# Two transformer blocks on one core: buffers at new places, cross attention in a new order, and small products moved

## The reference, cut to what matters

```python
x = x + 0.5 * swiglu(rmsnorm(x, ffn1_norm), ffn1_wgu, ffn1_wdown)
h = rmsnorm(x, mix_norm);  z = h @ w_in            # attention and convolution, gated, merged, @ w_out
x = x + merged @ w_out
x = x + 0.5 * swiglu(rmsnorm(x, ffn2_norm), ffn2_wgu, ffn2_wdown)
x = x + sigmoid(rmsnorm(x, ple_gate_norm) @ ple_gate_w) * rmsnorm(p @ ple_proj, ple_norm)
# second block
proj = rmsnorm(h, norm_mix_g) @ w_in_2             # q, k, v (short convolution), z, b, a, pool
h = h + concat(pool_mixer, gated_delta_rule) @ w_out_2
m = rmsnorm(mem, mem_norm_g)
q, k, v = rmsnorm(h, g) @ w_xq, m @ w_xk, m @ w_xv
h = h + (softmax(q k^T / 16) v) @ w_xo
h = h + relu(rmsnorm(h, g) @ w_up)**2 @ w_down
return rmsnorm(h, final_norm_g)
```

## Time and profile before

| | |
|---|---|
| median of 3 runs | 2119.24 us |
| the profiled execution: its time | 2118.75 us |
| its span | 2116.6 us |
| mean granted TensorE clock | 0.989 |
| HBM read and written | 241 MB, 33 MB |

### The profile page before, as it was taken

How to read it: one execution, slowest core, us unless ns; L and a number is a source line. 1 busy time by engine, 2 the same in 40 slices (tenths; PEclk the granted TensorE clock), 3 DMA queues, 4 the chain that set the end, 5 groups by cost and what they waited for, 6 DMA issues and landing times.

```text
span 2116.6 us, 25119 instructions
## 1 busy us (share of the span) xinstructions
PE 2056.2 (97%) x9682; PEld 1676.8 (79%) x9682; DVE 1230.4 (58%) x1737; ACT 831.3 (39%) x1268; POOL 5.9 (0%) x11
## 2 busy tenths in 40 slices
PE   7999999999899999999999999999998999999997
PEld 6888888887677787888888877789977778888886
DVE  5676575478998445554444565588563445544534
ACT  5444343334765443422222344334353433222211
POOL 0000000000000000000000000000000000000000
PEclk9999999999999999999999999999999999999998
DMA  7999884544234442333232321210143222322221
GB/s 255 297 296 304 271 291 162 184 162 154 100 114 146 159 149 93 127 100 100 90 99 93 99 88 60 70 41 16 34 136 100 96 74 98 101 90 99 90 100 60
DMA packets 80340, 275.09 MB, mean 130 GB/s; under 512 B 8928, under 2 KB 11360, under 8 KB 80224
## 3 DMA queue, kind: packets, MB, share of 16 engines
q1 hardware_dynamic: 79648, 272.72, 38.8%
q10 hardware_dynamic: 576, 0.79, 0.1%
HBM read 240.97 MB, written 32.51 MB: 129 GB/s over the span
## 4 chain that ended last, share of the span: by engine, by line
PE 87%; DVE 7%; ACT 3%; issue 2%; DMA 0%; DVEq 0%; ACTq 0%
PE ps L327 26%; PE ps L331 26%; PE ps L328 26%; DVE cacc L1697 2%; PE ps L349 1%; PE ps L647 1%; PE ps L640 1%; ACT whi L945 1%; PE ps L341 1%; PE ps L803 1%; PE ps L820 1%; DVE scr L2016 1%; DVE scr L1629 1%; DVE wlo L1587 0%; PE ps L480 0%
## 5 line engine op out<-in xcount | busy, mean ns | idle before, releaser
L327 PE MATMUL ps<-Hh,whi 128*128 128x512 f32 x1528 | 607.9, 398 | 23.6 <-DVE Hl L1615 11.1
L331 PE MATMUL ps<-Hh,wlo 128*128 128x512 f32 x1528 | 600.0, 393 | 2.5 <-DVE wlo L1587 2.5
L328 PE MATMUL ps<-Hl,whi 128*128 128x512 f32 x1528 | 599.3, 392 | 0.0
L945 ACT CAST whi<-raw 128x1024 fp32r<-128x1024 f32 (+3 forms) x352 | 350.4, 1001 | 361.4 <-PE ps L331 332.7
L1587 DVE TENSOR_TENSOR wlo<-raw,whi 128x1024 fp32r<-128x1024 f32 (+3 forms) x294 | 338.3, 1157 | 192.6 <-ACT whi L945 189.6
L327 PEld LDWEIGHTS ps<-Hh,whi 128*128 128x128 f32 x1528 | 289.6, 190 | 93.2 <-issue 15.9
L331 PEld LDWEIGHTS ps<-Hh,wlo 128*128 128x128 f32 x1528 | 289.4, 189 | 66.1 <-DVE wlo L1587 4.9
L328 PEld LDWEIGHTS ps<-Hl,whi 128*128 128x128 f32 x1528 | 289.4, 189 | 60.4 <-issue 1.7
L1697 DVE SCALAR_TENSOR_TENSOR cacc<-upad,gains,cacc 128x512 f32<-128x512 f32 x232 | 157.8, 744 | 0.0
L1653 DVE SCALAR_TENSOR_TENSOR x<-ps,x 128x512 f32<-128x512 f32 x80 | 55.3, 691 | 175.5 <-PE ps L331 175.4
L327 PE MATMUL ps<-f3Ah,whi 128*128 128x512 f32 x256 | 101.3, 396 | 0.0
(11 more groups left out here) (327 smaller groups left out, 2747.5 us busy)
## 6 DMA issues: line engine op xcount, KB each, us to landing
raw<-in_w SPq DMA_DIRECT2D x369, 512.0 KB, 4.0
low_parts<-lo SPq DMA_DIRECT2D x58, 512.0 KB, 4.7
wlo<-low_parts SPq DMA_DIRECT2D x58, 512.0 KB, 3.4
raw<-in_w SPq DMA_DIRECT2D x16, 384.0 KB, 3.0
raw<-in_w SPq DMA_DIRECT2D x17, 256.0 KB, 2.6
out<-x SPq DMA_DIRECT2D x8, 256.0 KB, 2.1
x<-in_x SPq DMA_DIRECT2D x5, 256.0 KB, 6.4
raw<-in_w SPq DMA_DIRECT2D x8, 128.0 KB, 2.0
```

The source lines that it names most:

```text
L327: e.matmul(out, h[:, kk, :], a, start=part != "last" and k + kk == 0, stop=False)
L328: e.matmul(out, h[:, kk, :], c, start=False, stop=False)
L331: ins = e.matmul(out, lo[:, kk, :], a, start=False, stop=done)
L945: e.copy(whi[i % WS][:, 0:n], raw[i % RAWS][:, 0:n]).then_inc(*act.tick("whi", ("whi", i)))
```

## The change

It moves the stage buffers, gives `P` a second buffer, pairs two products at the start of mix2, reorders cross attention on all engines and shifts some norms' parts. No instruction's kind or size is changed.

```diff
 # places: 16 KB "LOW" right behind Hl (where raw and whi began), x and raw behind the PB region
         RAWS, WS = 3, 3
-        x = glob("x", [128, 8, T])
         Hh, Hl = glob("Hh", [128, 8, T], F32R), glob("Hl", [128, 8, T], F32R)
-        raw = [glob(f"raw{i}", [128, 1024]) for i in range(RAWS)]
+        LOW = cursor[0]
+        cursor[0] += 16384
         whi = ...
         wlo = ...
+        PB = cursor[0]
+        cursor[0] += 83584
+        x = glob("x", [128, 8, T])
+        raw = [glob(f"raw{i}", [128, 1024]) for i in range(RAWS)]
...
-        A_hi = {t: [at(f"{t}Ah{i}", PB + 32768 * i, ...) for i in range(2)] ...}
-        A_lo = {t: [at(f"{t}Al{i}", PB + 32768 * i + 16384, ...) for i in range(2)] ...}
+        A_hi = {t: [at(f"{t}Ah0", LOW, ...), at(f"{t}Ah1", PB + 16384, ...)] ...}
+        A_lo = {t: [at(f"{t}Al0", PB, ...), at(f"{t}Al1", PB + 32768, ...)] ...}
...
-        q, aoh = at("q", QB, ...), at("aoh", QB, ...)
+        q, aoh = at("q", LOW, ...), at("aoh", LOW, ...)
...
+        Xm, LT = at("Xm", LOW, ...), at("LT", LOW + 8192, ...)
...
+        Yph, Ypl = at("Yph", LOW, ...), at("Ypl", o_TT, ...)
+        Ydh, Ydl = at("Ydh", LOW + 8192, ...), at("Ydl", PB + 8 * 2064, ...)
...
-        P = ph2("P", [128, 4, MEM])
+        P = [ph2(f"P{i}", [128, 4, MEM]) for i in range(2)]
...
-        axh, axl = ph2("axh", ...), ph2("axl", ...)
+        axh, axl = at("axh", LOW, ...), ph2("axl", ...)

 # TensorE
+            def gemm_two(keys, name, cols, xh, xl, xn):
+                made = []
+                for key, c in zip(keys, cols):
+                    take(key)
+                    made.append((key, *piece(name, 0, 8, [(c, 128)])))
+                    ends[key] = len(pieces)
+                for tiles in (range(7), (7,)):
+                    for key, i, h, lo in made:
+                        ...   # the three matmuls of each of these tiles, with gemm's waits
...
                 gemm(("pl", j), "ple_proj", ...)
-                if j == 0:
+                if j == 2:
                     norm_columns("f2")
-                if j == 1:
+                if j == 4:
                     norm_R("f2")
...
-            conv4(4)
+            gemm_two([("cv", 4), ("cv", 5)], "w_in_2", [1024, 1152], Hh, Hl, "mix2")
             norm_columns("mix2")
-            conv4(5)
+            conv4(6)
             norm_R("mix2")
-            conv4(6)
             conv4(7)
...
             q_x(2)
+            q_x(3)
             norm_columns("mem", 2)
-            q_x(3)
-            norm_R("mem", 2)
             k_x(0)
             k_x(1)
-            q_x(4)
-            v_x(0, {1: lambda: scores_x(0), 2: lambda: q_x(5)})
+            norm_R("mem", 2)
             k_x(2)
             k_x(3)
-            turn_x(0)
-            scores_x(1)
+            scores_x(0)
+            v_x(0, {1: lambda: scores_x(1), 3: lambda: turn_x(0)})
+            turn_x(1)
+            q_x(4)
             pv_x(0)
+            q_x(5)
+            pv_x(1)
             k_x(4)
             k_x(5)
             q_x(6)
-            turn_x(1)
             scores_x(2)
             q_x(7)
-            pv_x(1)
             k_x(6)
             k_x(7)
             turn_x(2)
             v_x(1, {1: lambda: scores_x(3)})
+            turn_x(3)
             pv_x(2)
-            turn_x(3)
             pv_x(3)

 # SyncE
                 for m, i in enumerate(early_pieces()):
-                    weights(m + 4)
+                    weights(m + 6)
...
+            sp.wait_ge("kept", early_pieces()[-1])      # ahead of the mask's load

 # ScalarE: f1 and f3
                         if f == 0:
                             deviation(name, 4, 1.0 / D)
+                            weights(ends[tag, "u", f] + 3)
                             norm_R(name, prev)
-                        if tag == "f1":
+                        if tag == "f1" and f:
                             make_early(2)
 # ScalarE: deviation("f2") at j == 3 and norm_R("f2") at j == 5 (both were at 1)
 # ScalarE: soft_x(h) waits for the transposes of head h - 2, not h - 1
 # ScalarE: cross attention (v0 = ends["xk", 3])
+            weights(v0 + 3)
+            soft_x(0)
+            weights(v0 + 4)
+            soft_x(1)
+            weights(v0 + 5)
+            turn_x(0)
+            weights(v0 + 6)
+            v_x(0)
+            turn_x(1)
+            weights(v0 + 8)
+            q_x(4)
+            pv_x(0)
...
 # VectorE: f1
                     after(("f1", "u", f))
-                    make_early(2)
+                    if f:
+                        make_early(2)
+                    else:
+                        weights(ends["f1", "u", f] + 3)
                     glu("f1", f, final=f == 21)
 # VectorE: reciprocal("f2") at j == 3 (was 0); reciprocal("k") behind conv4_in(1) (was behind conv4_in(2))
 # VectorE: the maximum and the scaling of the softmax are two functions, casts between them
+            for j in range(4):
+                after(("xk", j))
+                k_x(j)
+            soft_x(0)
+            weights(v0 + 3)
+            soft_x(1)
+            weights(v0 + 4)
+            scale_x(0)
+            weights(v0 + 5)
+            scale_x(1)
+            weights(v0 + 8)
+            pv_x(0)
...
```

More of the change, by code:

```diff
@@ L168, in build @@
         cacc = [at(f"cacc{i}", PB + 50176 + 2048 * i, [128, T]) for i in range(2)]
-        QB = PB + 54272
-        q, aoh = at("q", QB, [128, 8, T]), at("aoh", QB, [128, 8, T], F32R)
+        QB = PB + 37888
+        q, aoh = at("q", LOW, [128, 8, T]), at("aoh", LOW, [128, 8, T], F32R)
         kd = at("kd", QB + 22528, [128, T])
@@ L200, in build @@
         zt = ph2("zt", [128, 4, T])
-        o_LT = off[0]
-        LT = ph2("LT", [128, 4, 4, 128])
+        Xm, LT = at("Xm", LOW, [128, 4, 4, 128]), at("LT", LOW + 8192, [128, 4, 4, 128])
         Tm = ph2("Tm", [128, 4, 4, 128])
@@ L225, in build @@
         mem = at("mem", off[0], [128, 8, MEM])
-        P = ph2("P", [128, 4, MEM])
+        P = [ph2(f"P{i}", [128, 4, MEM]) for i in range(2)]
         PX = [ph2(f"PX{i}", [128, 2, T]) for i in range(2)]
-        axh, axl = ph2("axh", [128, 8, T], F32R), ph2("axl", [128, 8, T], F32R)
+        axh, axl = at("axh", LOW, [128, 8, T], F32R), ph2("axl", [128, 8, T], F32R)
         small_at, small_next = {}, [0]
@@ L336, in gemm @@
                 ends[(*key, "first") if part == "first" else key] = len(pieces)
+            def gemm_two(keys, name, cols, xh, xl, xn):
[6 more added lines that the diff above has]
+                    for key, i, h, lo in made:
+                        out = ps(key)[:, :]
+                        pe.wait_ge("whi", i)
+                        for k in tiles:
+                            pe.wait_ge("hi", xn, k)
+                            pe.wait_ge("lo", xn, k)
+                            e.matmul(out, h[:, k, :], xh[:, k, :], start=k == 0, stop=False)
+                            e.matmul(out, h[:, k, :], xl[:, k, :], start=False, stop=False)
+                            pe.wait_ge("wlo", i)
+                            ins = e.matmul(out, lo[:, k, :], xh[:, k, :], start=False, stop=k == 7)
+                        if k == 7:
+                            ins.then_inc(*pe.tick("gemm", ("piece", i), ("gemm", key)))
             def columns(key, src, into, nb=4, at_=0):
@@ L1509, in scalar_program @@
             q_x(2)
-            deviation("mem", 2, 1.0 / D)
             after(("xq", 3))
             q_x(3)
-            norm_R("mem", "mix2", MEM)
+            deviation("mem", 2, 1.0 / D)
             after(("xk", 0))
             after(("xk", 1))
-            after(("xq", 4))
+            norm_R("mem", "mix2", MEM)
+            after(("xk", 2))
+            after(("xk", 3))
+            v0 = ends["xk", 3]
+            weights(v0 + 3)
[8 more added lines that the diff above has]
+            weights(v0 + 8)
             q_x(4)
-            soft_x(0)
-            after(("xq", 5))
+            pv_x(0)
+            weights(v0 + 9)
             q_x(5)
[L1521 to L1529, removed]
+            pv_x(1)
+            weights(v0 + 12)
             q_x(6)
-            turn_x(1)
-            after(("xq", 7))
+            soft_x(2)
+            weights(v0 + 13)
             q_x(7)
[L1534 to L1537, removed]
+            weights(v0 + 15)
             turn_x(2)
-            weights(ends["xk", 7] + 3)
+            weights(v0 + 16)
             soft_x(3)
-            after(("xv", 1))
+            weights(v0 + 18)
             v_x(1)
+            turn_x(3)
+            weights(v0 + 19)
             pv_x(2)
-            turn_x(3)
             pv_x(3)
@@ L2066, in vector_program @@
             conv4_in(1)
+            reciprocal("k", 16)
             conv4(1)
@@ L2069, in vector_program @@
             conv4_in(2)
-            reciprocal("k", 16)
             conv4(2)
@@ L2311, in soft_x @@
             def soft_x(h):
-                mx, nm, sm, rd = (cols((w, h), 4) for w in ("xmx", "xnm", "xsm", "xrd"))
```

(37 more changed lines are left out.)

42 lines of the change are left out of this document (20 added, 22 removed).

## The result

The changed kernel takes 2070.82 us (median of 4 runs, 2069.99 to 2072.88) for 2119.47 of the kernel before beside it: ratio 0.9766, 95% interval 0.9749 to 0.9783. The forecast was 2083, with 2070 to 2097. So the direction was right and the time lies at the low edge. The profiled span went from 2116.6 to 2067.3 us: 49.3 us gained where 36.2 were forecast. Measured once more, beside the last experiments, it took 2070.66 and 0.9766 [0.9753, 0.9779].

The account below looks back on a forecast made before the run. TensorE, busy 97% of the span, was taken as the bound. Terms 7.7 + 7.1 + 1.4 + 4.3 + 15.7 = 36.2 us off 2118.75 gave 2082.6, with the median's half microsecond 2083; range 2070 to 2097.

Parts of the forecast that it names:

- Places: Products whose high parts move from the low buffer LOW: 0.2267 us a matmul instead of 0.2333, 7.7 us gained.
- The signs that the prediction named for itself: In f1's down products, 24 matmuls in 5.49 us for block 0 and 5.60 for block 1, among other signs.
- The rival that had the larger size (2075): Address limit above the new low part of PB, so places are worth more: 2075 us, chance 0.13.
- the one that had places worth nothing: Pace follows something other than address, so moving buffers gains nothing: 2090 us, chance 0.13.
- Start of f1: First FFN's start: a cast put ahead of the norm's copy ends the fifth product's wait, 7.1 us gained.
- Norm of f2: Second FFN's norm: columns and spread placed behind later products cover the wait for the sum of squares, 1.4 us gained.
- Mix2: Second mixer's start: paired products fill a wait, k's reciprocal comes a round earlier, pi1 starts sooner, 4.3 us gained.
- Cross attention: New order there removes waits for casts queued behind softmax and the lower clock after them, 15.7 us gained.
- the in-order queues: Rival: ScalarE's casts behind waits for TensorE give back 8 us of cross attention, mix2 at 0.7: 2094 us, chance 0.10.
- the early loads: Rival: f1's early loads come late in each of 21 steps, slower than before, 2126 us at 2.5 us; chance 0.04.

Follow-up runs that it names:

- a1: The kernel before with the stage region PB 32 bytes higher, nothing else: 2100.44 us, ratio 0.9907.
- b1: The changed kernel with the first FFN's start as before (loads 4 pieces ahead, early work at the first step, no third early cast): 2078.78 us, ratio 0.9804.
- b3: The changed kernel with mix2's pair undone and k's reciprocal and the second FFN's norm where they were: 2075.42 us, ratio 0.9791.
- v1: The changed kernel with the weight casts of the second mixer's first products made sooner on ScalarE and VectorE: 2058.64 us, ratio 0.9712.
- b2: The changed kernel with cross attention in the old order on all engines and one buffer for P: 2088.73 us, ratio 0.9853.
- b4: The changed kernel with everything the products' matmuls read pushed up by the same 32 bytes: 2073.36 us, ratio 0.978.
- c1: The kernel before with weights, Hh and Hl brought to 96 bytes past a multiple of 128, where PB already stood: 2105.5 us, ratio 0.993.
- a2: The changed kernel with PB moved up by 32 bytes: 2084.51 us, ratio 0.9829.
- a4: The changed kernel with weights whi and wlo 32 bytes past a multiple of 128, PB and all behind it at 64: 2111.97 us, ratio 0.996.
- a3: The changed kernel with PB moved up by 64 bytes: 2081.8 us, ratio 0.9815.

## Why the prediction was right and wrong, by its steps

**Places: the step that failed.** "What is left is the place of the moving operand: Hh and Hl are low in the arena". Place it was, but not height. Two buffers differ in more than how high they lie, and I compared only that; the sizes in the code would have shown PB at 96 bytes past a multiple of 128 from the weights. Height gave 1216 matmuls and 7.7 us. With the distance as cause all that read PB count: the down products of f1, f2 and f3 with both halves (8 outputs x 76 hidden tiles x 3 = 1824), attention's and convolution's projections (384), w_out, the gate, w_xo and the second mixer's output (192 each), v_x (96) and p's product (48), some 3120, x 0.0067 = 21 us (a little less, since the second mixer's output hardly gained). The signs that the prediction named for itself, 5.49 us for 24 matmuls in block 0 and 5.60 in block 1, came out as 5.44 in both. The same 32 bytes measured alone gave 18.1 us of span (a1). So the term was short by some 10 to 13 us, most or all of the 13.1 by which the sum was short. The rival that had the larger size (2075) had the wrong mechanism as well; the one that had places worth nothing is excluded by a1. The Trainium skill's "TensorE: Matmul & The Clock Gate", section Back-to-back issue gap, gives the gap by the number of columns and names no start address. The 215.8 ns that the prediction took from it are there the gap of a matmul by itself, and a stream of 512 columns is given some 131 ns, which no run here shows: for 512 columns the runs have 226.7 ns where the two operands stand well and 228.9 to 233.3 otherwise.

**Start of f1: right.** Forecast 7.1; the fifth product takes 5.44 us (33.63 to 39.07) and no wait is left between 25 and 50 us. The casts came at 22.14, 32.89 and 42.20, forecast 22.5, 33.3 and 42.6. Undoing it cost 8.8 us of span, 1.4 more than wait and clock together (7.4); 0.9 of that lies ahead of 14 us, in the first product, whose fifteenth matmul starts at 13.97 us in b1 and at 12.98 in the changed kernel because its matmuls still take 0.63 us each until 13.5 us where the changed kernel's take 0.39. The edit begins to act later.

**Norm of f2: right.** Forecast 1.4, measured 1.7 between the kernels. b3 shows what the step left out: such a wait may pull the clock down behind it, and is then worth 3.3.

**Mix2: right in its course, too high in its price.** Forecast 4.3; 3.75 against before, but only 2.3 in b3, and about 1 of its span: the other 1.5 between before and b3 (86.71 and 85.24) came without the pair, at a mean clock of 0.94 for 0.90. The new wait ahead of ab was forecast at 4.6 and is 4.65; the spread goes 19.4 us behind the first product's start where 18.4 were worked out (1280.2 less 1261.8). Of the 1.0 between them, 0.9 is the growth of a wait that the pair can't fill, of which the prediction didn't speak: the low part of tile 6, 0.95 us in the kernel before and 1.85 now. The pair fills the one for tile 7. k's spreads don't wait, pi1 waits for the bank. What I took as given, that the cast must stand behind R's chain, was the order of the code, not a need: v1 moves it and gains 12.0 us.

**Cross attention: right.** Forecast 15.7; 15.4 by b2. One wait is left, forecast at 0.6:

```profile
1652.67 7.13 PE L840 MATMUL ps<-PX,vm 128*128 128x512 f32 x16 [0.48 <-ACT vm L1520]
```

**Sum.** Measured parts: places 18.1 (a1), start 8.8 (b1), norm and mix2 5.6 (b3), order 15.4 (b2) = 47.9 of 49.3 us; 1.4 stays without a place. These mix spans and stretches; by spans alone it is 18.1 + 8.8 + 4.4 + 18.0 = 49.3, and that this closes to the tenth is luck, since b1's and b2's spans hold 0.9 and 1.6 us that their edits didn't cause.

That the time fell inside the range is luck too. The low edge, 2070, was put together from a limit of height that isn't there and mix2's full head start, which didn't come. The two rivals in which something was given back, by the in-order queues or by the early loads, did not come about.

## What to carry to other kernels

Look at the start addresses of both operands of a matmul: where the profile has two paces for one shape, bring both moving halves to a multiple of 512 bytes from the weights, as the fast products here have it, before anything else is tuned; here it was 0.9% for 32 bytes. A multiple of 128 may not be enough. When a wait names a cast, ask when its inputs and its buffer were ready, and where it stands in its engine's program: ab's cast could run 13.7 us sooner, 14.3 against the start of its stretch. And a wait is to be priced with the product behind it, since the clock may fall with it.

## What the runs showed of the hardware

A stream of 128x128 by 128x512 fp32r matmuls runs at 0.2267 us each where both moving halves start a multiple of 512 bytes from the weights, wherever they stand themselves (remainders 0, 32 and 96 modulo 128 tried: a1, b4, c1). It runs at 0.2333 where the distance is 32 bytes more or less (before, a2, a4), and at 0.2289 where the moving operand is 64 bytes further (a3). Halves at different distances give 0.2317 (0 and 32), 0.2319 (0 and 64) and about 0.231 to 0.233 (0 and 128, the second mixer's output). That holds although the weight loads (189 ns) lie beside the matmuls. With 256 moving columns (k_x, where mh moves and the weights stand) there is no such gain, rather a small loss: 0.118 us in the kernel before, 0.120 in the changed one and in a1, b4 and c1, 0.117 to 0.118 in a2 and a3. What in the memory makes it is open.

Whether the clock falls behind a short wait isn't told by the wait alone: the 4.65 us ahead of ab cost a further 24 x (0.338 - 0.2267) = 2.7 us, 1.73 us in b3 brought 0.90, 1.68 us in the kernel before nothing. In v1 it falls with no wait of note ahead: after the k spreads and 12 products of four columns pi0 runs at 0.302 a matmul, the stretch around it:

```profile
1302.00:1310.00 8.00, 8.00 (x34) 6.55 (x33) 4.01 (x6) 1.54 (x4) 0.00 (x0) 0.79 0.22 68
```
